# Value products of a head pair: once for all four query blocks instead of once per query block

## What is computed

```python
qa, ka, va, qb, kb, vb, ... = project(h, w_in, ...)   # 8 heads of 64 for each mixer
logits = jnp.einsum('bthd,bshd->bhts', q, k).astype(jnp.float32) * (HEAD_DIM ** -0.5)
logits = logits + (Fq - Fk)            # mixer B; mixer A: ALiBi distance and the top-k mask instead
logits = jnp.where(kpos <= qpos, logits, MASK_VALUE)
p = jax.nn.softmax(logits, axis=-1).astype(v.dtype)
o = jnp.einsum('bhts,bshd->bthd', p, v)            # the value products
```

## Time and profile before

| | us |
|---|---|
| median of 3 runs (lowest, highest) | 966.08 (965.3, 968.95) |
| the profiled execution | 965.95 |
| span of its trace, first to last instruction | 964.2 |
| TensorE busy | 935.7 (97%) |
| VectorE, ScalarE, GpSimd busy | 491.4, 392.3, 138.2 |
| TensorE busy with the value products | 25.0 |
| mean granted TensorE clock | 0.986 |

### The profile page before, as it was taken

One profiled execution on the slowest core, in us unless ns is written; L12 is line 12 of the kernel. 1 busy time (PEld: TensorE's weight loads), 2 busy tenths in 40 slices (PEclk: granted clock), 3 DMA queues, 4 the chain that ended last, 5 costly groups with the idle time before them and its releaser, 6 DMA issues.

```text
span 964.2 us, 19815 instructions
## 1 busy us (share of the span) xinstructions
PE 935.7 (97%) x7546; PEld 858.8 (89%) x7546; DVE 491.4 (51%) x1154; ACT 392.3 (41%) x813; POOL 138.2 (14%) x139
## 2 busy tenths in 40 slices
PE   8799999999999999999999999999999999999997
PEld 7588668788878878997899989999999999999997
DVE  3553768963736797731277447445322354442332
ACT  3254556654656766333233214443211234331111
POOL 4100232232335674200000000000000000000000
PEclk9889999998999999999999998999999999999999
DMA  9646674255324564967223331332333333333212
GB/s 319 204 110 193 181 249 138 94 165 162 113 77 154 160 184 130 293 212 245 68 80 99 89 88 45 88 87 87 92 99 94 87 88 87 89 99 96 87 44 89
DMA packets 176233, 124.54 MB, mean 129 GB/s; under 512 B 14739, under 2 KB 152019, under 8 KB 176164
## 3 DMA queue, kind: packets, MB, share of 16 engines
q1 hardware_dynamic: 176034, 123.50, 42.3%
q10 hardware_dynamic: 130, 0.10, 0.0%
HBM read 116.99 MB, written 6.59 MB: 128 GB/s over the span
## 4 chain that ended last, share of the span: by engine, by line
PE 71%; issue 19%; DVE 5%; ACT 2%; POOL 1%; POOLq 0%; ACTq 0%; DVEq 0%
PE bank L952 19%; PE bank L953 18%; PE bank L954 18%; PE bank L1056 2%; PE bank L1033 2%; PE bank L1012 2%; PE bank L859 2%; PE bank L1042 2%; PE bank L1074 1%; PE bank L881 1%; PE bank L1018 1%; PE bank L1097 1%; DVE sel L1881 1%; PE bank L1087 1%; POOL w_lo L813 0%
## 5 line engine op out<-in xcount | busy, mean ns | idle before, releaser
L952 PE MATMUL bank<-h_hi,w_hi 128*128 128x260 f32 x1360 | 397.1, 292 | 8.6 <-DVE h_lo L1765 6.5
L953 PE MATMUL bank<-h_lo,w_hi 128*128 128x260 f32 x1360 | 388.1, 285 | 0.0
L954 PE MATMUL bank<-h_hi,w_lo 128*128 128x260 f32 x1360 | 387.6, 285 | 0.0
L952 PEld LDWEIGHTS bank<-h_hi,w_hi 128*128 128x128 f32 x1360 | 259.8, 191 | 31.2 <-issue 23.0
L953 PEld LDWEIGHTS bank<-h_lo,w_hi 128*128 128x128 f32 x1360 | 260.0, 191 | 0.0
L954 PEld LDWEIGHTS bank<-h_hi,w_lo 128*128 128x128 f32 x1360 | 259.9, 191 | 0.0
L952 PE MATMUL bank<-u_hi,w_hi 128*128 128x260 f32 x512 | 145.2, 284 | 0.0
L2222 DVE TENSOR_TENSOR w_lo<-raw,w_hi 128x1024 fp32r<-128x1024 f32 x62 | 76.0, 1225 | 135.1 <-ACT w_hi L1641 135.1
L953 PE MATMUL bank<-u_lo,w_hi 128*128 128x260 f32 x512 | 144.8, 283 | 0.0
L954 PE MATMUL bank<-u_hi,w_lo 128*128 128x260 f32 x512 | 144.8, 283 | 0.0
L1641 ACT ACTIVATE w_hi<-raw 128x1024 fp32r<-128x1024 f32 x62 | 65.4, 1055 | 140.3 <-PE bank L954 140.3
(11 more groups left out here) (316 smaller groups left out, 1162.2 us busy)
## 6 DMA issues: line engine op xcount, KB each, us to landing
raw<-in_w_in SPq DMA_DIRECT2D x44, 512.0 KB, 4.1
part<-in_w_ada SPq DMA_DIRECT2D x32, 512.0 KB, 5.5
raw<-in_w_up SPq DMA_DIRECT2D x32, 512.0 KB, 4.1
raw<-in_w_down SPq DMA_DIRECT2D x32, 512.0 KB, 4.1
ada<-in_w_ada SPq DMA_DIRECT2D x4, 2048.0 KB, 13.6
kv<-in_cache_k_b SPq DMA_DIRECT2D x16, 256.0 KB, 4.4
qbc<-q_d SPq DMA_DIRECT2D x16, 256.0 KB, 5.2
kv<-in_cache_k_a SPq DMA_DIRECT2D x16, 256.0 KB, 4.5
```

Of the source, the lines that this page charges most:

```text
L952: mm(out, hi[:, k, :], x_h, start=first and k == ks[0], stop=False)
L953: mm(out, hi[:, k, :], x_l, start=False, stop=False)
L954: end = mm(out, lo[:, k, :], x_h, start=False, stop=last and k == ks[-1])
```

## The change

All value products of a pair are made at once, in slot 2 of iteration row p + 2 for pair p, after the projection (and `mod_part`) and ahead of `to_tokens(p + 2, 0)`. They go key block by key block: key block kb is multiplied with all query blocks from kb on, so the moving operand has 512, 384, 256 and 128 columns. Eight products take the place of twenty. For this `p_t` holds the turned probabilities of a whole pair, 15 KB a partition, laid out so that for each key block the query blocks lie side by side; the kernel is built with `dynamic_dma_scratch_size=1024`, which leaves more of the on-chip memory to its tiles.

```diff
-        p_t = new("p_t", [P, 2, 2, QB, P])
+        p_t = new("p_t", [P, 2, QB + 1, (QB - 1) * P])
...
-                    sp.wait_ge(pv_done, N_UNITS // 2)
+                    sp.wait_ge(pv_done, N_PAIRS)
...
-            def values(U):
-
-                p, _, qb = unit(U)
-                pe.wait_ge(pt_ready, U + 2)
-                if qb == 0:
-                    pe.wait_ge(v_ready, p + 1)
-                    if p >= 1:
-                        pe.wait_ge(o_lo_ready, p)
-                for kb in range(qb + 1):
+            def values(p):
+
+                pe.wait_ge(pt_ready, 8 * (p + 1))
+                pe.wait_ge(v_ready, p + 1)
+                if p >= 1:
+                    pe.wait_ge(o_lo_ready, p)
+                for kb in range(QB):
                     for hh in range(2):
                         rows = slice(64 * hh, 64 * hh + 64)
-                        last = mm(bank[7][rows, qb * P:(qb + 1) * P], v_tok[:, p % 2, kb, rows],
-                                  p_t[:, qb % 2, hh, kb, :], start=kb == 0, stop=kb == qb)
+                        turned = p_t[:, hh].rearrange("p r c -> p (r c)")
+                        last = mm(bank[7][rows, kb * P:SEQ], v_tok[:, p % 2, kb, rows],
+                                  turned[:, QB * kb * P:QB * kb * P + (QB - kb) * P], start=kb == 0, stop=kb == QB - 1)
                 last.then_inc(pv_done, 1)
...
+                if s == 2 and p >= 2:
+                    values(p - 2)
                 if p < N_PAIRS:
                     if s == 2:
                         to_tokens(p, 0)
...
-                if 0 <= U - 5 < N_UNITS and U % 2:
-                    values(U - 5)
...
-                if U >= 4:
-                    act.wait_ge(pv_done, U // 2 - 1)
-                A(p_t[:, qb % 2, hh, 0:qb + 1, :], bank[6][:, 0:width(qb)].rearrange("p (k c) -> p k c", k=qb + 1),
+                if U % 8 == 0 and U >= 8:
+                    act.wait_ge(pv_done, U // 8)
+                r, c = divmod(qb, QB - 1)
+                A(p_t[:, hh, r:r + qb + 1, c * P:c * P + P], bank[6][:, 0:width(qb)].rearrange("p (k c) -> p k c", k=qb + 1),
                   ACT.Copy).then_inc(pt_ready, 1)
...
-                act.wait_ge(pv_done, QB * (p + 1))
+                act.wait_ge(pv_done, p + 1)
```

More of the change, by code:

```diff
@@ L847, in _ @@
             pool.wait_ge(prod_dve, len(DVE_KEYS) - 1)
-            pool.wait_ge(pv_done, N_UNITS // 2)
+            pool.wait_ge(pv_done, N_PAIRS)
             pool.memset(ptz[:, :, :], 0.0).then_inc(s_consts, 1)
@@ L1488, in store_v @@
                     act.wait_ge(v_stored, 16 * (p - 1))
-                    act.wait_ge(pv_done, QB * (p - 1))
+                    act.wait_ge(pv_done, p - 1)
                 A(v_tok[:, p % 2], bank[2][:, :].rearrange("p (t c) -> p t c", t=QB), ACT.Copy).then_inc(v_ready, 1)
             def round_o(p):
-                act.wait_ge(pv_done, QB * (p + 1))
+                act.wait_ge(pv_done, p + 1)
                 A(o_hi[:, p, 0:SEQ], bank[7][:, :], ACT.Copy).then_inc(o_hi_ready, 1)
@@ L2277 @@
     from concourse.bass_utils import run_bass_kernel_spmd as _run
-    nc = _bacc.Bacc("TRN2", target_bir_lowering=False, num_devices=1)
+    nc = _bacc.Bacc("TRN2", target_bir_lowering=False, num_devices=1, dynamic_dma_scratch_size=1024)
     arrays, aps = {}, {}
```

## The result

The changed kernel takes **974.51 us** (median of 5 runs, 973.49 to 976.7) against 966.08 before, also a median of 5; the ratio is 1.0084, 95% interval 1.0068 to 1.0101. It is slower by about 8 us. The forecast was 963.0 with a range of 958.2 to 967.5, so it was wrong, and the time lies beyond the range.

A forecast was written before the change was run, and what follows sets the result against it. The prediction took TensorE as the bound (71% of the span), with VectorE deciding in some attention stretches. Of 7.9 us saved on TensorE, row shifts summing to -2.96 would arrive, taking 965.95 to 963.0 us, range 958.2 to 967.5.

The forecast's parts named there:

- The price of the new group: Slot 2: ten 128-column blocks plus one fixed 0.15 us make 2.28 us, 2.37 from row 6 on.
- its arrival in full: Slot 2 ahead of the queries' turn: everything behind that turn is late by 2.28 us against slot 1.
- the view that columns and not records cost: Value products: a block costs 0.22 us at 128 columns, 0.213 at 512; the skill's per-matmul saving of 2.4 us not counted.
- Slot 6 of row 7: Sign: TensorE's wait there, 1.92 us before for the normalized keys, becomes 3 us and more.
- new waits of TensorE for VectorE or ScalarE in rows 3 to 6: Attention rows 3 to 6: if such waits appear, the forecast is wrong; no size given.
- the account: TensorE's shift summed over attention rows 1 to 9, negative is earlier: row 2 +0.45, row 3 -1.65, total -2.96 us.
- the turn of unit 15: Sign at (3,1): TensorE waits 2 us and more there, where it waited 0.8.
- slot 1 of row 6: Sign: it starts some 3 to 4 us earlier than before.
- removing a group gives back 0.48, 0.70, 0.92 and 1.13 us: Old groups for query blocks 0 to 3, slots 5, 7, 1 and 3: TensorE saves 3.23 us a pair.
- Its row 6: Row 6: -0.55 us, with VectorE's idle ahead of slot 4 (0.99) below slot 3's 1.13 and 0.17 taken for slot 5.
- the forecast's sentence on the tiling mode: Between full-array and half-array products on TensorE: changing the mode drains it, 0.09 us each way.
- VectorE carries the delay: Rival: VectorE bounds slot 2 to next slot 1; rows 2 to 7 keep +1.36 each; 974.1 us, chance 0.07.

The follow-up runs named there:

- narrow_slot2: The changed kernel with twenty value products of 128 columns, query block by query block, all in slot 2; 977.83 us, ratio 1.0115.
- before_short: The kernel before with each value group cut to its first key block, nothing moved; 963.69 us, ratio 0.9959.
- behind_turn: The changed kernel with the value group behind the turn of the queries, `to_tokens(p, 0)`, still in slot 2; 975.11 us, ratio 1.0088.
- no_mask_wait: The changed kernel without GpSimd's wait for VectorE's masks at the start of rows 1 to 5; 976.66 us, ratio 1.0114.
- after_512_only: The changed kernel with its slot 2 group cut to the first key block's two products of 512 columns; 965.79 us, ratio 0.9977.
- layout_only: The kernel before with only the changed memory layout: 7 KB a partition more behind `p_t` and the smaller DMA scratch; 966.37 us, ratio 1.0005.
- before_plus_group: The kernel before with a second value group of the new form added in slot 2 of rows 2 to 9, nothing removed; 984.61 us, ratio 1.0179.

## Why the prediction was wrong

**What held.** The price of the new group (2.28 and 2.37 forecast; 2.30 and 2.40 measured, 2.5 in rows 8 and 9), its arrival in full, and the view that columns and not records cost: `narrow_slot2` and the changed kernel have nearly the same steps. Slot 6 of row 7 has the wait of over 3 us that I named, 3.2 in the list of waits above (before: the earlier trace rows). The forecast also said that new waits of TensorE for VectorE or ScalarE in rows 3 to 6 would prove it wrong, and they did. Other signs that it named did not come: row 2 costs 2.0 us where the account had 0.45, TensorE waits at the turn of unit 15 for 0.81 us as before and not for 2, and slot 1 of row 6 starts 3.6 us later (apart from the start-up), not 3 to 4 earlier.

**The step that failed** is "removing a group gives back 0.48, 0.70, 0.92 and 1.13 us" wherever TensorE does not wait. I asked of each slot whether the chain is on TensorE and whether TensorE shows idle time, and took a "no" to the second as slack. The account had 18.6 us of insertion and 21.6 of removals, -2.96. (Its row 6 names 0.99 as the most that slot 3 can bring, but adds up to -0.55 only with 1.13; with 0.99 it is -0.41, too small a slip to matter.) Measured in the attention, without the one new half-clock stretch in it (1.6 us), is +6.8: 19.0 of insertion, so 12.2 of removals. The missing 9.4 us went into waits like these, in the order of the rows:

*Slot 1 of rows 2 and 3, all of 0.92 lost twice.* The first product behind the old group needs `w_lo`. GpSimd before, then TensorE before (start us, us):

```profile
154.44 2.39 POOL L813 TENSOR_TENSOR w_lo<-raw,w_hi 128x1024 fp32r<-128x1024 f32 x1 [14.38 <-DVE fdiag L2072]
```

```profile
156.09 0.88 PE L1056 MATMUL bank<-p_t,v_tok 128*64 128x128 f32 x12
156.93 0.36 PE L952 MATMUL bank<-h_hi,w_hi 128*128 128x260 f32 x1
```

`w_lo` ends at 154.44 + 2.39 = 156.83, and the product starts at 156.93. There is no wait to be seen, yet the value products end just when the weights come. In the changed kernel:

```profile
156.81 2.39 POOL L813 TENSOR_TENSOR w_lo<-raw,w_hi 128x1024 fp32r<-128x1024 f32 x1 [14.38 <-DVE fdiag L2072]
...
193.97 2.35 POOL L813 TENSOR_TENSOR w_lo<-raw,w_hi 128x1024 fp32r<-128x1024 f32 x1 [15.39 <-DVE fdiag L2072]
```

```profile
159.30 0.36 PE L952 MATMUL bank<-h_hi,w_hi 128*128 128x260 f32 x1 [0.78 <-issue]
...
196.43 0.36 PE L952 MATMUL bank<-h_hi,w_hi 128*128 128x260 f32 x1 [0.87 <-issue]
```

Again 0.10 us behind the end of `w_lo` (159.20 and 196.32), with the group's time turned into idle time. The sequencer's own records, which the views of TensorE's busy time leave out, had the wait before the change too; line 991 is the last of the projection's waits, and the record ends 0.03 us after the semaphore that `w_lo` sets (ns: start, length, what, line):

```
before   155462, 1413, EVENT_SEMAPHORE, 991
after    157750, 1498, EVENT_SEMAPHORE, 991
```

*Slot 3 of rows 2 to 5, 0.6 of 1.13 lost four times.* ScalarE's copy for `mod_turn_part` (line 1018) takes 0.60 us; the old group lay over it. Before, ScalarE and TensorE:

```profile
166.53 0.60 ACT L1508 ACTIVATE mod_row<-bank 128x512 f32<-128x512 f32 x1 [0.58 <-PE bank L1012]
```

```profile
166.65 1.09 PE L1056 MATMUL bank<-p_t,v_tok 128*64 128x128 f32 x16
167.67 1.06 PE L1018 MATMUL bank<-fold_p,mod_row 128*128 128x9 f32 x8
```

The copy ends at 167.13 and its reader starts at 167.67: about 0.5 us of slack under a group of 1.13. After, at the same place:

```profile
171.02 0.33 PE L1042 MATMUL bank<-ident,lg 128*128 128x128 f32 x1
171.81 0.39 PE L1018 MATMUL bank<-fold_p,mod_row 128*128 128x9 f32 x2 [0.46 <-ACT mod_row L1508]
```

The table has the steps -0.52, -0.51, -0.48 and -0.51, and `before_short` the same ones for a removal half as large: the slack and no more.

*Slots 3 and 5 of rows 6 to 8, most of it given back.* Here the removal arrives at slot 4 (-1.17) and the next wait takes +0.83 and +0.72. The chain of the changed kernel in row 6 (start us, us, what) leaves TensorE right where slot 3's projection ends:

```profile
314.01 0.13 PE bank L954
...
314.17 0.38 ACT z L1432
...
316.15 0.95 ACT w_hi L1400
...
317.24 0.31 POOL w_lo L813
317.55 2.15 issue
...
319.74 1.65 POOL rs L807
...
321.41 0.70 DVE tok L1936
322.12 0.04 issue
322.16 0.65 PE bank L1086 x4
```

ScalarE makes the next weights, GpSimd their low part, and only behind it the inverse root that the normalized keys wait for. Before, the same root ended at 313.94, the keys were normalized at 314.65 and turned back at 315.13 without a wait, 0.48 us of slack for the 1.6 us of two groups:

```profile
312.30 1.64 POOL L807 TENSOR_TENSOR rs<-ms,neghalf 128x8 f32<-128x8 f32 x1
```

```profile
315.13 0.60 PE L1087 MATMUL bank<-ident,tok 128*128 128x128 f32 x4
```

VectorE's idle of 0.99 us at the earlier trace rows, which I used as the bound, was not the shortest path. The wait that came of it, in TensorE's timeline:

```profile
322.16 0.65 PE L1086 MATMUL bank<-ident,tok 128*128 128x128 f32 x4 [1.24 <-DVE tok L1936]
```

VectorE's 128 x 8 operation of line 1927 ahead of the root also lies beside `w_lo`. In the changed kernel, the one for the queries, which has nothing beside it, and the one for the keys:

```profile
311.72 0.17 DVE L1927 TENSOR_SCALAR ms<-ms 128x8 f32<-128x8 f32 x1
...
318.34 1.32 DVE L1927 TENSOR_SCALAR ms<-ms 128x8 f32<-128x8 f32 x1
```

Before, the one for the keys took 0.90 us, also beside `w_lo`. It hardly matters here, since the root stands behind `w_lo` on GpSimd anyway.

*The rest.* The groups of slots 5 and 7 of rows 1 and 2 were counted as lost, rightly. In slot 7 of row 4 a side step now waits 0.8 us (line 1123), and in row 8 the turns of the probabilities wait for ScalarE (1.8 us for one, line 1042), which the earlier trace rows had shown for slot 5 but not for slot 3. The sum 19.0 of insertion, less 25.8 to 26.5 of removals, plus 12.2 of new waits is 4.7 to 5.4, and 1.4 to 2.1 us are missing up to the measured 6.8. The starts of the two traces, compared product by product, show where such time hides. The view of waits shows less than a wait costs: a product's record lasts 0.28 us while the next one starts 0.12 us behind it, so the first part of a wait lies under the record of the product ahead. In slot 3 of rows 2 to 5 a removal moves TensorE by 0.50 us where the same one brings 1.20 in rows 6 and 7: 0.70 is lost, and the view shows 0.46 of idle time. In slot 1 of row 2 0.98 is lost where it shows 0.78, in slot 6 of row 6 1.40 where it shows 1.24. Some losses are too short for the list, as 0.27 us at the turned keys of slot 6 in each of rows 3 and 4.

The same comparison shows that the removed groups were priced too low. Where nothing waits behind it, a removal moves TensorE by 0.54, 0.76, 0.98 and 1.20 us, each 0.06 more than forecast, so the way from half arrays back to the full array costs about 0.08 us and not 0.02 (an estimate from these steps; the forecast's sentence on the tiling mode says 0.09 us each way, but its sum has only 0.02 for the way back). The 32 groups then weigh at least 27.8 us, and the waits ate at least 15.6 of them. The list shows 12.2; its twelve additional waits with about 0.2 us hidden in each make 2.4 of the difference, also an estimate, and about 1 us stays open.

**The rival that came close in time** ("VectorE carries the delay", 974.1) was right in its number and wrong in its cause: `behind_turn` takes the delay away and the time stays. Its account had +1.36 in each of rows 2 to 7 and almost nothing in rows 8 and 9. The traces have 2.0, 0.8, 0.9, -0.1, 0.9 and 1.7 in rows 2 to 7 and 1.8 in row 8, and the start-up (+2.5) and the MLP (-2.9) happen to cancel. That the sum agrees is luck.

**The clock and the MLP.** The profiled execution has three half-clock stretches that the one of before has not. Windows of the changed kernel (PE, PEld, DVE, ACT, POOL busy, clock):

```profile
24.00:27.40 3.40, 3.40 (x17) 0.67 (x10) 1.95 (x4) 0.12 (x1) 2.49 (x7) 0.50 1.04 399
354.80:358.30 3.50, 3.50 (x12) 1.67 (x13) 1.44 (x8) 1.70 (x4) 0.46 (x1) 0.54 1.01 346
480.60:484.60 4.00, 4.00 (x22) 4.00 (x23) 0.23 (x1) 0.22 (x1) 0.00 (x0) 0.59 0.44 131
```

They cost about 1.6 us each. The first lies in the start-up, whose instructions the change leaves as they are; `no_mask_wait` and `after_512_only` have the change and not that stretch. The second comes behind row 7's wait. Every run that takes the groups out of the odd slots or shortens them has it; of the three that leave them alone only `layout_only` has it. So it may belong to what the removals cost; these runs can't decide that. The third is in six of the eight experiments, removals and insertions alike, but not in `layout_only`, `narrow_slot2` or the kernel before. On the other side, the MLP's products follow each other every 119.3 ns in the changed kernel (and in `no_mask_wait`) and every 120.3 in the one before and the other experiments; between 607 and 940 us that gives back 2.7 of the 2.9 us. What decides either stays open. Together they are +5.6 and -2.9 us of one execution; the comparison with `before_plus_group` and `before_short`, whose sums go the same way, says that they did not decide the sign.

**A version that beats both** was not found, and the numbers don't point to one of this form: the new group costs 19.0 us where it stands, the old ones are worth 12.2 to the program (the difference of 19.0 and the measured 6.8; no run removes them whole and adds nothing).

## What to carry to other kernels

An engine without idle time ahead of an instruction can still be waiting: work that ends just when the awaited result comes is free, and its removal only uncovers the wait. Before pricing a removal, take for each thing behind it the end of its producer (here `w_lo` 156.83 against 156.93) and count only the gap between that and the consumer's start. Work gathered from slots with such cover into one without it pays its full length there, so fewer instructions can cost more time; adding the new part alone and shortening the old part alone, in two runs, showed it here.

## What the runs showed of the hardware that I had not expected

- Some VectorE instructions stand still beside a GpSimd `tensor_tensor` of 128 x 1024: a `TENSOR_SCALAR` of 512 columns took 2.51 instead of 0.43 us, two additions with both inputs in SBUF 3.49 instead of 1.29, a `TENSOR_SCALAR` on 128 x 8 1.32 instead of 0.17. `MAX8`, `MATCH_REPLACE8` and `TENSOR_REDUCE` kept their 0.68 or 0.69 us beside it.
- A group of half-array products costs the same in products of 128 as of 512 columns (`narrow_slot2` against the changed kernel, steps of 2.33 and 2.29 us), within 0.04 us.
- Half-clock stretches of 3.4 us, about 1.5 us of loss each, appear and go at places that an edit doesn't touch (24, 355 and 481 us).
